# Inverse units of a chunked DeltaNet scan: level masks ahead on GpSimd, products carried by ScalarE, products and Relus spread over steps

## The chip, the cores and the metric

One core of one Trainium2 chip runs the whole kernel. The metric is the device time of one execution in microseconds (us), before and after the change. TensorE (PE) multiplies matrices into PSUM; VectorE (DVE), ScalarE (ACT) and GpSimd (POOL) work elementwise; SyncE (SP) and others issue the transfers. Each engine runs its own queue in order and waits on semaphores for the others.

## What is computed

One layer of a hybrid backbone over 128 context and 512 latent tokens in fp32: a first SwiGLU feed-forward net, a mixer with two head groups (gated DeltaNet and differential attention), the output projection, a second feed-forward net and a final norm. The change lies in the gated DeltaNet, in the part that solves the triangular system of each chunk:

```python
kk = jnp.einsum('bhncd,bhnsd->bhncs', kc, kc)
a_mat = jnp.where(strict, bc[..., :, None] * kk * decay, 0.0) + jnp.eye(CHUNK, dtype=jnp.float32)
rhs = jnp.concatenate([bc[..., None] * vc, (bc * jnp.exp(gc))[..., None] * kc], axis=-1)
sol = lax.linalg.triangular_solve(a_mat, rhs, left_side=True, lower=True, unit_diagonal=True)
...
qk = jnp.where(incl, jnp.einsum('bhncd,bhnsd->bhncs', qc, kc) * decay, 0.0)
```

There are 8 heads, two scan directions, and 5 token tiles of 128 (one of context, four latent).

## The kernel before

The kernel runs in stages: first feed-forward net, input projection and convolution, attention units, then **inverse units**, the scan (with parts of the output projection between), and the second feed-forward net. The inverse units lie between about 815 and 989 us.

An inverse unit makes the inverse of the 128x128 matrices of one token tile and four heads; both directions share it, since the strictly lower part serves one and the strictly upper part the other. There are 10 units u. Each goes through 20 steps k = 0 to 19, and starts at global step `MAKE_START[u]` (0, 4, 8, 13, 20, 24, 28, 33, 40, 44). Four sets of buffers c = u % 4 (`m_t`, `x_w`, `t_cols`, `tt_cols`; the last two sets have the name `spare` in the trace) and two PSUM banks each are used in turn, r = u // 4. `make_schedule` yields, for every global step, the events of that step with k None (attention tail, k and v transposed, scan beginnings) and then the steps of the units in order of u. All four engines write their queues by this one schedule; it sets the order within a queue, and semaphores (`t_pe`, `t_dve`, `t_act`, `t_pool`, with `PE_T`, `DVE_T`, `ACT_T`, `POOL_T` counts a unit) do the rest.

The steps of a unit before the change:

- k = 0: ScalarE fills `tt_cols` with beta (L1269, 4 instructions). k = 1: ScalarE's Relu of the decay rows of both directions, which a transfer brought (L1277, 4 for `x_w`, 4 for `t_cols`).
- k = 2: GpSimd adds the two (L2286); TensorE computes k*k and q*k of four heads (`products`, L2860). k = 3: ScalarE's exponential (L1282). k = 4: GpSimd multiplies beta in (L2289).
- k = 5: VectorE multiplies the products by the decays, into `m_t` (L2094) and `p_all` (L2096). k = 6: ScalarE copies the 32x32 diagonal blocks of `m_t` to `x_w[:, 1]` (L1286).
- k = 7: VectorE makes the inverse of level 0 (L2100, L2103), the transpose (L2114) and the two masked sides (L2116).
- Levels n = 1 to 4, k = 6 + 2n and 7 + 2n: TensorE multiplies the blocks with one side (`inner_first`, L2869, into PSUM); VectorE masks the product with the level's pattern into `x_w[:, 2]` (L2107); TensorE multiplies it with the other side (`inner_second`, L2876); VectorE subtracts it (L2111), transposes (L2114) and masks the sides (L2116).
- k = 16 to 19: the levels of 32 and 64 columns (`outer_first` L2884, `outer_own` L2896, `outer_second` L2902, `outer_turned` L2909, `last_first` L2920, `last_second` L2928), with ScalarE's negated copies (L1290, L1293), VectorE's L2120 and ScalarE's copies to `t_all` (L1297, L1303).

SyncE brings the decay rows of the next unit of a buffer set (`decays_spread`, L684) when the old unit is done. From global step 49 on GpSimd also masks the inverses for the scan (L2254, L2262), and from 54 on ScalarE prepares the scan (L1225) and the Silu of z (L1256, with table loads).

## Time and profile before

| | before |
|---|---|
| median of 3 runs | 1546.77 us (1543.21 to 1547.66) |
| the profiled execution | 1546.29 us, its span 1544.5 us |
| TensorE busy | 1458.2 us (94%) |
| VectorE busy | 1009.0 us (65%) |
| ScalarE busy | 620.6 us (40%) |
| GpSimd busy | 107.1 us (7%) |

The shares are means over stages. A stretch has to be read by itself: its busy times first, then what each engine waited for last. Times in the rows are microseconds from the start of the span, unless marked ns.

### The profile page before, as it was taken

How to read it: one execution, taken by the hardware profiler on the slowest of the kernel's cores; microseconds unless marked ns; L12 is line 12 of the kernel's file. 1: busy time of each engine (PE TensorE's matmuls, PEld its weight loads, DVE VectorE, ACT ScalarE, POOL GpSimd, SP SyncE). 2: the span in 40 equal slices, each digit the busy share in tenths (PEclk: the TensorE clock that was granted, in tenths of full speed). 3: DMA queues.
4: the chain of work that ended last, by engine and by line, in shares of the span. 5: the costliest groups of instructions: out<-in, count | busy, mean ns of one | idle time of the engine just before them, and what ended most of it. 6: DMA issues, size and time to landing. Idle time of an engine off the chain costs nothing.

```text
span 1544.5 us, 31492 instructions
## 1 busy us (share of the span) xinstructions
PE 1458.2 (94%) x12718; PEld 1350.8 (87%) x12718; DVE 1009.0 (65%) x1893; ACT 620.6 (40%) x1240; POOL 107.1 (7%) x88
## 2 busy tenths in 40 slices
PE   7899999999999999999996777899999999999998
PEld 2899999999999999887785556799999999998886
DVE  4977777777465747552886675478877777753333
ACT  4522222221122533442556555554544444444223
POOL 0000000000000000020002113553000000000000
PEclk9999999999999999998998776999999999999999
DMA  9344454445244222212101110111122223222222
GB/s 346 104 143 150 139 159 149 149 137 163 95 137 143 76 68 69 55 55 56 42 1 63 45 39 11 36 56 55 55 69 82 81 86 91 82 68 69 82 69 96
DMA packets 174589, 141.70 MB, mean 92 GB/s; under 512 B 8464, under 2 KB 156437, under 8 KB 173461
## 3 DMA queue, kind: packets, MB, share of 16 engines
q1 hardware_dynamic: 151652, 117.63, 24.5%
q10 hardware_dynamic: 22833, 22.59, 4.7%
q8 instruction: 77, 1.26, 0.3%
q14 instruction: 27, 0.22, 0.0%
HBM read 136.75 MB, written 3.45 MB: 91 GB/s over the span
## 4 chain that ended last, share of the span: by engine, by line
PE 83%; DVE 10%; issue 2%; ACT 2%; SPq 1%; DMA 1%; DVEq 0%; ACTq 0%
PE ps L2317 15%; PE ps L2318 14%; PE ps L2319 14%; PE ps L2469 5%; PE ps L2467 5%; PE ps L2468 5%; PE ps L2539 3%; PE ps L2537 3%; PE ps L2538 3%; PE ps L2959 1%; PE ps L2747 1%; PE ps L2768 1%; PE ps L2973 1%; PE ps L2944 1%; DVE tt_cols L2116 1%
## 5 line engine op out<-in xcount | busy, mean ns | idle before, releaser
L2317 PE MATMUL ps<-h_hi,w_lo 128*128 128x320 f32 x1152 | 366.5, 318 | 12.2 <-DVE h_lo L1445 4.5
L2318 PE MATMUL ps<-h_lo,w_hi 128*128 128x320 f32 x1152 | 358.5, 311 | 0.0
L2319 PE MATMUL ps<-h_hi,w_hi 128*128 128x320 f32 x1152 | 358.3, 311 | 0.0
L1398 DVE TENSOR_TENSOR w_lo<-w_raw,w_hi 128x1024 fp32r<-128x1024 f32 x120 | 148.1, 1236 | 233.3 <-ACT w_hi L742 233.0
L2317 PEld LDWEIGHTS ps<-h_hi,w_lo 128*128 128x128 f32 x1152 | 218.5, 190 | 19.6 <-issue 8.1
L2318 PEld LDWEIGHTS ps<-h_lo,w_hi 128*128 128x128 f32 x1152 | 218.9, 190 | 0.8 <-issue 0.2
L2319 PEld LDWEIGHTS ps<-h_hi,w_hi 128*128 128x128 f32 x1152 | 218.5, 190 | 0.0
L742 ACT CAST w_hi<-w_raw 128x1024 fp32r<-128x1024 f32 x120 | 125.5, 1047 | 198.8 <-PE ps L2319 109.3
L1532 DVE SCALAR_TENSOR_TENSOR ada_acc<-ada_ffn,cond,ada_acc 128x256 f32<-128x256 f32 x392 | 161.8, 479 | 1.2
L2317 PE MATMUL ps<-act_hi,w_lo 128*128 128x320 f32 (+1 forms) x352 | 108.9, 309 | 2.1 <-DVE mods L1561 2.1
L2318 PE MATMUL ps<-act_lo,w_hi 128*128 128x320 f32 (+1 forms) x352 | 108.5, 308 | 0.0
L2319 PE MATMUL ps<-act_hi,w_hi 128*128 128x320 f32 (+1 forms) x352 | 108.5, 308 | 0.0
L2467 PE MATMUL ps<-h_hi,w_lo 128*128 128x320 f32 x304 | 94.0, 309 | 0.6 <-ACT sumsq L905 0.6
L2469 PE MATMUL ps<-h_hi,w_hi 128*128 128x320 f32 x304 | 94.1, 310 | 0.0
L2468 PE MATMUL ps<-h_lo,w_hi 128*128 128x320 f32 x304 | 93.9, 309 | 0.0
L2537 PE MATMUL ps<-w_hi,act_hi 128*128 128x512 f32 x220 | 87.4, 397 | 0.0
L2539 PE MATMUL ps<-w_hi,act_lo 128*128 128x512 f32 x220 | 86.8, 395 | 0.0
L2538 PE MATMUL ps<-w_lo,act_lo 128*128 128x512 f32 x220 | 86.8, 394 | 0.0
L835 ACT CAST act_hi<-scratch 128x640 f32 (+1 forms) x22 | 16.0, 728 | 148.4 <-DVE scratch L1587 148.4
L2317 PEld LDWEIGHTS ps<-act_hi,w_lo 128*128 128x128 f32 x352 | 66.1, 188 | 2.4 <-issue 2.3
L2318 PEld LDWEIGHTS ps<-act_lo,w_hi 128*128 128x128 f32 x352 | 66.1, 188 | 0.1
L2319 PEld LDWEIGHTS ps<-act_hi,w_hi 128*128 128x128 f32 x352 | 66.1, 188 | 0.0
(425 smaller groups left out, 2909.2 us busy)
## 6 DMA issues: line engine op xcount, KB each, us to landing
w_raw<-in_w_ffn_in SPq DMA_DIRECT2D x64, 512.0 KB, 3.9
w_raw<-in_w_ffn_out SPq DMA_DIRECT2D x44, 512.0 KB, 3.7
ada_ffn<-in_w_ada ACTq DMA_DIRECT2D x43, 512.0 KB, 4.0
w_raw<-in_w_in SPq DMA_DIRECT2D x28, 512.0 KB, 3.7
ada_ffn<-in_w_ffn_in SPq DMA_DIRECT2D x20, 512.0 KB, 3.8
ada_k<-in_w_ada SPq DMA_DIRECT2D x8, 1024.0 KB, 10.6
ada_ffn<-in_w_ada SPq DMA_DIRECT2D x13, 512.0 KB, 3.4
w_raw<-in_w_out SPq DMA_DIRECT2D x8, 512.0 KB, 3.4
```

What stands on the lines that cost most here:

```text
L742: nc.scalar.copy(w_hi[s if slot is None else slot], w_raw[s][:]).then_inc(w_hi_ready, 1)
L1398: nc.vector.tensor_tensor(w_lo[at], w_raw[s][:], w_hi[at].bitcast(F32), ALU.subtract)\
L1532: ins = nc.vector.scalar_tensor_tensor(a, w, col, a, op0=ALU.mult, op1=ALU.add)
L2317: nc.tensor.matmul(out, lo, xh, start=start, stop=False)
L2318: nc.tensor.matmul(out, hi, xl, start=False, stop=False)
L2319: return nc.tensor.matmul(out, hi, xh, start=False, stop=stop)
L2467: nc.tensor.matmul(out, lo, xh, start=start and k == 0, stop=False, skip_group_check=not start)
L2468: nc.tensor.matmul(out, hi, xl, start=False, stop=False, skip_group_check=not start)
L2469: ins = nc.tensor.matmul(out, hi, xh, start=False, stop=k == 3, skip_group_check=not start)
L2537: nc.tensor.matmul(out, lo, wh, start=first, stop=False)
L2538: nc.tensor.matmul(out, hi, wl, start=False, stop=False)
L2539: ins = nc.tensor.matmul(out, hi, wh, start=False, stop=last)
```

## The change

`MAKE_START` and the 20 steps stay. The change

- moves TensorE's `products` from one lump in step 2 to one head in each of the steps 1 to 4,
- moves the second half of the Relus from step 1 to step 2, the exponential from step 3 to step 4, and `p_all` (L2096) from step 5 to step 6,
- lets ScalarE copy the diagonal blocks to `t_cols[:, 2]`, and lets GpSimd multiply them in step 6 with the patterns of levels 1 and 2, and 3 and 4, into `x_w[:, 0:4]` (two instructions),
- lets `inner_first` read those masked blocks, so that its product needs no mask. ScalarE copies it from PSUM to `t_cols[:, 3]` in steps 8, 10, 12 and 14, and VectorE's L2107 is gone.

```diff
 Z_TOTAL = [sum(Z_FIRST[:v + 1]) + sum(Z_SECOND[:v + 1]) for v in range(len(Z_FIRST))]
 Z_DONE = [min(v for v, n in enumerate(Z_TOTAL) if n >= 4 * g + 4) for g in range(2 * HB)]
 
-PE_T, DVE_T, ACT_T, POOL_T = 15, 23, 9, 2
+PE_T, DVE_T, ACT_T, POOL_T = 15, 19, 13, 4
 MAKE_ORDER = [0, 1, 4, 2, 3]
 OUT_ORDER = [0, 2, 3, 1, 4]
 OUT_EARLY = 3
...
             i = CONST_NAMES.index("pack0") * P + PACKED.index(name) * SUB
             return cst[:, i:i + SUB][:, None, :].broadcast_to([P, n, SUB])
 
+        def packed_pair(name, n):
+            i = CONST_NAMES.index("pack0") * P + PACKED.index(name) * SUB
+            return cst[:, i:i + 2 * SUB].rearrange("p (l n) -> p l n", n=SUB)[:, :, None, :].broadcast_to([P, 2, n, SUB])
+
         def unit_ident(a):
             i = CONST_NAMES.index("pack0") * P
             return cst[a:a + SUB, i:i + SUB]
...
                     ins.then_inc(t_act[c], 1)
                 if k == 1:
                     act.wait_ge(chain_in[c], 32 * r + 32)
-                    for d, x in ((0, x_w[c]), (1, t_cols[c])):
-                        q = 8 * d + 4 * g
-                        for h in range(4):
-                            ins = nc.scalar.activation(x[:, h, :], x[:, h, :], ACT.Relu,
-                                                       bias=gc[:, t, q + h:q + h + 1], scale=-1.0)
-                        ins.then_inc(t_act[c], 1)
-                if k == 3:
+                if k in (1, 2):
+                    d, x = ((0, x_w[c]), (1, t_cols[c]))[k - 1]
+                    q = 8 * d + 4 * g
+                    for h in range(4):
+                        ins = nc.scalar.activation(x[:, h, :], x[:, h, :], ACT.Relu,
+                                                   bias=gc[:, t, q + h:q + h + 1], scale=-1.0)
+                    ins.then_inc(t_act[c], 1)
+                if k == 4:
                     act.wait_ge(t_pool[c], r * POOL_T + 1)
                     nc.scalar.activation(x_w[c][:], x_w[c][:], ACT.Exp, scale=-1.0).then_inc(t_act[c], 1)
                 if k == 6:
-                    act.wait_ge(t_dve[c], r * DVE_T + 2)
+                    act.wait_ge(t_dve[c], r * DVE_T + 1)
                     for a in range(0, P, SUB):
-                        ins = nc.scalar.copy(heads4(x_w[c][a:a + SUB, 1, :], SUB), m_t[c][a:a + SUB, :, a:a + SUB])
+                        ins = nc.scalar.copy(heads4(t_cols[c][a:a + SUB, 2, :], SUB), m_t[c][a:a + SUB, :, a:a + SUB])
                     ins.then_inc(t_act[c], 1)
+                if k in (8, 10, 12, 14):
+                    act.wait_ge(t_pe[c], r * PE_T + k - 6)
+                    nc.scalar.copy(t_cols[c][:, 3, :], ps[:, 2 * c, 0:P]).then_inc(t_act[c], 1)
                 if k == 16:
                     act.wait_ge(t_pe[c], r * PE_T + 10)
                     nc.scalar.activation(x_w[c][:, 2, :], ps[:, 2 * c, 0:P], ACT.Copy, scale=-1.0).then_inc(t_act[c], 1)
...
                     act.wait_ge(t_pe[c], r * PE_T + 14)
                     nc.scalar.activation(x_w[c][:, 2:4, :].rearrange("p a n -> p (a n)"), ps[:, 2 * c, 0:256],
                                          ACT.Copy, scale=-1.0).then_inc(t_act[c], 1)
-                    act.wait_ge(t_dve[c], r * DVE_T + 23)
+                    act.wait_ge(t_dve[c], r * DVE_T + 19)
                     for a in range(0, P, DK):
                         ins = nc.scalar.copy(heads4(t_all[a:a + DK, t, g, :], P)[:, :, a:a + DK],
                                              heads4(ps[a:a + DK, 2 * c + 1, 256:512], DK))
...
                 nc.vector.tensor_tensor(out, out if s in (0, 3, 4) else oq[b], ps[:, 4 + b, 256:512], ALU.add).then_inc(c_dve[b], 1)
 
 
+            def by_pair(x):
+                return x.rearrange("p (h e) n -> p e h n", e=2)
+
+            def by_pair_of(x):
+                return x.rearrange("p e (h n) -> p e h n", n=P)
+
             for k, c, r, t, g in make_schedule():
                 if k is None:
                     if c == 4:
...
                 if k == 5:
                     dve.wait_ge(t_pe[c], pe0 + 1)
                     dve.wait_ge(t_pool[c], r * POOL_T + 2)
-                    for_heads = [x.rearrange("p (h e) n -> p e h n", e=2)
-                                 for x in (m_t[c][:], tt_cols[c][:], heads4(p_all[:, t, g, :], P), x_w[c][:])]
-                    nc.vector.tensor_tensor(for_heads[0], ps[:, bank:bank + 2, 256:512].rearrange("p e (h n) -> p e h n", n=P),
-                                            for_heads[1], ALU.mult).then_inc(t_dve[c], 1)
-                    nc.vector.tensor_tensor(for_heads[2], ps[:, bank:bank + 2, 0:256].rearrange("p e (h n) -> p e h n", n=P),
-                                            for_heads[3], ALU.mult).then_inc(t_dve[c], 1)
+                    nc.vector.tensor_tensor(by_pair(m_t[c][:]), by_pair_of(ps[:, bank:bank + 2, 256:512]), by_pair(tt_cols[c][:]),
+                                            ALU.mult).then_inc(t_dve[c], 1)
+                if k == 6:
+                    nc.vector.tensor_tensor(by_pair(heads4(p_all[:, t, g, :], P)), by_pair_of(ps[:, bank:bank + 2, 0:256]),
+                                            by_pair(x_w[c][:]), ALU.mult).then_inc(t_dve[c], 1)
                 if k == 7:
                     dve.wait_ge(t_act[c], act0 + 5)
-                    nc.vector.tensor_tensor(heads4(t_now, SUB), heads4(x_w[c][:, 1, :], SUB), packed("level0", 4),
+                    nc.vector.tensor_tensor(heads4(t_now, SUB), heads4(t_cols[c][:, 2, :], SUB), packed("level0", 4),
                                             ALU.mult).then_inc(t_dve[c], 1)
                     dve.wait_ge(t_dve[c], dve0 + 3)
                     nc.vector.tensor_tensor(heads4(t_now, SUB), heads4(t_now, SUB), packed("ident", 4), ALU.add).then_inc(t_dve[c], 1)
                 n, part = divmod(k - 6, 2)
-                if 1 <= n <= 4 and part == 0:
-                    dve.wait_ge(t_pe[c], pe0 + 2 * n)
-                    nc.vector.tensor_tensor(heads4(x_c, SUB), heads4(ps[:, bank, 0:P], SUB), packed(f"level{n}", 4),
-                                            ALU.mult).then_inc(t_dve[c], 1)
                 if 1 <= n <= 4 and part == 1:
                     dve.wait_ge(t_pe[c], pe0 + 1 + 2 * n)
                     nc.vector.tensor_tensor(t_now, t_now, ps[:, bank + 1, 0:P], ALU.subtract).then_inc(t_dve[c], 1)
                 if 0 <= n <= 4 and part == 1:
-                    dve.wait_ge(t_dve[c], dve0 + 4 + 4 * n)
+                    dve.wait_ge(t_dve[c], dve0 + 4 + 3 * n)
                     nc.vector.transpose(t_cols[c][:, 0, :], t_now).then_inc(t_dve[c], 1)
-                    dve.wait_ge(t_dve[c], dve0 + 5 + 4 * n)
+                    dve.wait_ge(t_dve[c], dve0 + 5 + 3 * n)
                     nc.vector.tensor_tensor(subs(t_sides), subs(t_pair), packed(f"sides{n + 1}", 8), ALU.mult).then_inc(t_dve[c], 1)
                 if k == 17:
                     dve.wait_ge(t_pe[c], pe0 + 13)
...
                 if k == 2:
                     pool.wait_ge(t_act[c], r * ACT_T + 3)
                     nc.gpsimd.tensor_tensor(x_w[c][:], x_w[c][:], t_cols[c][:], ALU.add).then_inc(t_pool[c], 1)
+                if k == 6:
+                    pool.wait_ge(t_act[c], r * ACT_T + 5)
+                    pool.wait_ge(t_dve[c], r * DVE_T + 2)
+                    for n in (1, 3):
+                        nc.gpsimd.tensor_tensor(x_w[c][:, n - 1:n + 1, :].rearrange("p l (h n) -> p l h n", n=SUB),
+                                                t_cols[c][:, 2:3, :].rearrange("p l (h n) -> p l h n", n=SUB)
+                                                .broadcast_to([P, 2, 4, SUB]),
+                                                packed_pair(f"level{n}", 4), ALU.mult).then_inc(t_pool[c], 1)
                 if k == 4:
                     pool.wait_ge(t_act[c], r * ACT_T + 4)
                     nc.gpsimd.tensor_tensor(tt_cols[c][:], tt_cols[c][:], x_w[c][:], ALU.mult).then_inc(t_pool[c], 1)
...
                 rows = slice((h % 2) * DK, (h % 2) * DK + DK)
                 return pre[rows, which + 2 * g + h // 2, t * P:(t + 1) * P]
 
-            def products(t, g, c):
-
-                for h in range(4):
-                    rows = slice((h % 2) * DK, (h % 2) * DK + DK)
-                    at = 2 * g + h // 2
-                    both = pre[rows, at:at + 5:4, t * P:(t + 1) * P]
-                    out = heads4(ps[:, 2 * c + h % 2, :], P)[:, h // 2:h // 2 + 3:2, :]
-                    ins = nc.tensor.matmul(out, qk(t, g, h, 4), both, start=True, stop=True)
-                ins.then_inc(t_pe[c], 1)
+            def products(t, g, c, h):
+
+                rows = slice((h % 2) * DK, (h % 2) * DK + DK)
+                at = 2 * g + h // 2
+                both = pre[rows, at:at + 5:4, t * P:(t + 1) * P]
+                out = heads4(ps[:, 2 * c + h % 2, :], P)[:, h // 2:h // 2 + 3:2, :]
+                ins = nc.tensor.matmul(out, qk(t, g, h, 4), both, start=True, stop=True)
+                if h == 3:
+                    ins.then_inc(t_pe[c], 1)
 
             def blocks_of(x, a, h):
                 return x[a:a + SUB, h * SUB:(h + 1) * SUB]
 
-            def inner_first(c):
+            def inner_first(c, n):
                 for h in range(4):
                     for a in range(0, P, SUB):
-                        ins = nc.tensor.matmul(blocks_of(ps[:, 2 * c, 0:P], a, h), blocks_of(x_w[c][:, 1, :], a, h),
+                        ins = nc.tensor.matmul(blocks_of(ps[:, 2 * c, 0:P], a, h), blocks_of(x_w[c][:, n - 1, :], a, h),
                                                blocks_of(tt_cols[c][:, 0, :], a, h), start=True, stop=True)
                 ins.then_inc(t_pe[c], 1)
 
             def inner_second(c):
                 for h in range(4):
                     for a in range(0, P, SUB):
-                        ins = nc.tensor.matmul(blocks_of(ps[:, 2 * c + 1, 0:P], a, h), blocks_of(x_w[c][:, 2, :], a, h),
+                        ins = nc.tensor.matmul(blocks_of(ps[:, 2 * c + 1, 0:P], a, h), blocks_of(t_cols[c][:, 3, :], a, h),
                                                blocks_of(tt_cols[c][:, 1, :], a, h), start=True, stop=True)
                 ins.then_inc(t_pe[c], 1)
 
...
                         attention_part(n // 2, [n % 2])
                     continue
                 pe0, dve0, act0 = r * PE_T, r * DVE_T, r * ACT_T
-                if k == 2:
+                if k == 1:
                     if r >= 1:
                         pe.wait_ge(t_act[c], act0)
                     elif c >= 1:
                         pe.wait_ge(kv_copied, 4 if c == 1 else 2 * NT + 2)
-                    products(t, g, c)
+                if 1 <= k <= 4:
+                    products(t, g, c, k - 1)
                 n, part = divmod(k - 6, 2)
                 if 1 <= n <= 4 and part == 0:
-                    pe.wait_ge(t_dve[c], dve0 + 2 + 4 * n)
-                    inner_first(c)
+                    pe.wait_ge(t_dve[c], dve0 + 3 + 3 * n)
+                    pe.wait_ge(t_pool[c], r * POOL_T + 3 + n // 3)
+                    inner_first(c, n)
                 if 1 <= n <= 4 and part == 1:
-                    pe.wait_ge(t_dve[c], dve0 + 3 + 4 * n)
+                    pe.wait_ge(t_act[c], act0 + 5 + n)
                     inner_second(c)
                 if k == 16:
-                    pe.wait_ge(t_dve[c], dve0 + 22)
+                    pe.wait_ge(t_dve[c], dve0 + 18)
                     outer_first(c)
                     outer_own(c)
                 if k == 17:
-                    pe.wait_ge(t_act[c], act0 + 6)
+                    pe.wait_ge(t_act[c], act0 + 10)
                     pe.wait_ge(t_pe[c], pe0 + 11)
                     outer_second(c)
                     pe.wait_ge(t_pe[c], pe0 + 12)
                     outer_turned(c)
                 if k == 18:
-                    pe.wait_ge(t_dve[c], dve0 + 23)
+                    pe.wait_ge(t_dve[c], dve0 + 19)
                     last_first(c)
                 if k == 19:
-                    pe.wait_ge(t_act[c], act0 + 7)
+                    pe.wait_ge(t_act[c], act0 + 11)
                     last_second(c)
 
             attention_part(1, [1])
```

## Rows read from the trace of the kernel before

**Rows 1.** Stretches: length; busy (x) PE, PEld, DVE, ACT, POOL; clock; DMA share; GB/s.
```profile
832.00:989.00 157.00, 114.00 (x4103) 92.39 (x4102) 96.00 (x243) 84.14 (x247) 40.68 (x32) 0.71 0.12 37
952.00:976.00 24.00, 21.76 (x568) 20.35 (x568) 10.22 (x30) 13.09 (x36) 5.03 (x5) 0.73 0.01 3
1100.00:1200.00 100.00, 98.10 (x666) 97.44 (x665) 80.26 (x124) 50.14 (x77) 0.00 (x0) 1.00 0.21 60
```

**Rows 2.** VectorE's waits, 832 to 989 us: waiter, releaser, total us, times, longest.
```profile
DVE t_cols L2111 <- PE ps L2876: 14.9, 10, 3.9
DVE spare L2107 <- PE ps L2869: 12.5, 11, 2.4
DVE spare L2111 <- PE ps L2876: 8.3, 6, 2.5
DVE x_w L2107 <- PE ps L2869: 7.8, 8, 1.8
```

**Rows 3.** Groups by line, 832 to 989 us: count | busy us, mean ns | idle before.
```profile
L2116 DVE TENSOR_TENSOR tt_cols<-t_cols,cst 128x256 f32<-128x256 f32 x30 | 18.7, 625 | 1.0
...
L2116 DVE TENSOR_TENSOR spare<-spare,cst 128x256 f32<-128x256 f32 x20 | 11.6, 579 | 0.7
...
L2107 DVE TENSOR_TENSOR x_w<-ps,cst 128x128 f32<-128x128 f32 x24 | 6.7, 285 | 8.0 <-PE ps L2869 7.8
...
L2107 DVE TENSOR_TENSOR spare<-ps,cst 128x128 f32<-128x128 f32 x16 | 4.6, 289 | 12.5 <-PE ps L2869 12.5
...
L1290 ACT ACTIVATE x_w<-ps 128x128 f32<-128x128 f32 x6 | 1.7, 277 | 9.3 <-PE ps L2884 9.3
```

**Rows 4.** Timeline, VectorE and TensorE, around 899 us: start, length, engine, line.
```profile
899.27 0.29 DVE L2107 TENSOR_TENSOR x_w<-ps,cst 128x128 f32<-128x128 f32 x1 [0.39 <-PE ps L2869]
899.57 0.29 DVE L2111 TENSOR_TENSOR t_cols<-t_cols,ps 128x128 f32<-128x128 f32 x1
...
899.02 1.10 PE L2876 MATMUL ps<-tt_cols,x_w 32*32 32x32 f32 x64
```

**Rows 5.** Timeline, VectorE and TensorE, 901 to 904 us, with a step 5.
```profile
901.24 0.42 DVE L2116 TENSOR_TENSOR tt_cols<-t_cols,cst 128x256 f32<-128x256 f32 x1
...
902.18 0.68 DVE L2096 TENSOR_TENSOR p_all<-ps,spare 128x512 f32<-128x512 f32 x1
902.78 0.48 DVE L2107 TENSOR_TENSOR x_w<-ps,cst 128x128 f32<-128x128 f32 x2
903.83 0.29 DVE L2111 TENSOR_TENSOR t_cols<-t_cols,ps 128x128 f32<-128x128 f32 x1 [0.57 <-PE ps L2876]
...
901.72 0.65 PE L2869 MATMUL ps<-tt_cols,x_w 32*32 32x32 f32 x32 [0.35 <-DVE tt_cols L2116]
903.12 1.08 PE L2876 MATMUL ps<-tt_cols,x_w 32*32 32x32 f32 x64 [0.74 <-DVE x_w L2107]
```

**Rows 6.** Timeline, TensorE and VectorE, a lump of products and the wait behind it.
```profile
872.69 2.08 PE L2860 MATMUL ps<-pre 64*128 64x256 f32 x8
...
876.37 0.29 DVE L2111 TENSOR_TENSOR spare<-spare,ps 128x128 f32<-128x128 f32 x1 [2.47 <-PE ps L2876]
```

**Rows 7.** Timeline, GpSimd and VectorE, 906 to 910 us.
```profile
906.66 1.27 POOL L2286 TENSOR_TENSOR spare<-spare 128x512 f32<-128x512 f32 x1 [8.26 <-ACT spare L1277]
...
906.84 1.37 DVE L2116 TENSOR_TENSOR spare<-spare,cst 128x256 f32<-128x256 f32 x1
```

**Rows 8.** Timeline, ScalarE: Relus, diagonal copies, and its queue before the scan.
```profile
823.53 1.26 ACT L1277 ACTIVATE t_cols<-t_cols,gc 128x128 f32<-128x128 f32 x4
...
883.37 1.22 ACT L1286 COPY x_w<-m_t 32x128 f32<-32x128 f32 x4
...
951.26 3.93 ACT L1225 ACTIVATE square<-k_tok,ekg 128x64 f32<-128x64 f32 x16
...
959.13 1.28 ACT L770 ACT_TABLE_LOAD   x1
```

**Rows 9.** The chain, 818 to 823 us: start, length, what.
```profile
818.95 3.37 DMA x_w<-decay_store
```

## Prediction

> **What bounds the kernel now.** I read the busy shares per stretch first. In a stretch that nothing here touches (1100 to 1200 us) TensorE is busy 98.1 of 100 us; the kernel is bound there by matmuls. In the stretch of the inverse units, 832 to 989 us, no engine is: TensorE 114.0 of 157 us, VectorE 96.0, ScalarE 84.1, GpSimd 40.7, and the granted clock is 0.71 on the mean, a mix of both levels [rows 1]. So this stretch is bound by latency: each of the four queues runs in order, step by step through the same schedule, and waits for its neighbours. What is saved on that round comes off the end one for one, because TensorE's dense work starts when it is over.
>
> Then VectorE's waits in it. 19 waits for the first product of a level (L2869) before the level mask L2107 come to 20.3 us, 16 for the second product (L2876) before the subtraction L2111 to 23.2 us; the longest waits of the two kinds are 2.4 and 3.9 us [rows 2]. Within the stretch 952 to 976 us TensorE is busy 21.8 of 24 us [rows 1]: it is the bound there, and no edit of this change shortens its work.
>
> **Part 1: the level masks leave VectorE.** 24 + 16 = 40 instructions L2107, 6.7 + 4.6 = 11.3 us busy, go away. What takes their place in the chain is a ScalarE copy of 128x128 from PSUM; the same shape from the same banks is L1290, 277 ns against 285 to 289 ns [rows 3]. The hop itself thus costs the same, if ScalarE is free. Is 11.3 us the gain? No, and one pair of steps shows it. VectorE masks the younger unit at 899.27 and subtracts for the older at 899.57; the older unit's second product started at 899.02, behind the first product of the younger [rows 4]. TensorE takes the products in order (first a, first b, second a), so with no mask VectorE would wait for second a, to about 899.6. Gain: nothing. The mask filled a gap.
>
> It gains where L2094/L2096 (step 5 of a young unit) stand ahead of the masks. The older units' masked sides end at 901.66 (901.24 + 0.42). VectorE runs L2096 at 902.18, both masks at 902.78, and only then can the two second products run (903.12 for 1.08 us), so L2111 starts at 903.83. The last first product had started at 901.72 and took 0.65 [rows 5]. With a copy by ScalarE the second product can run at 902.37, take about half of 1.08, and L2111 follows L2096 directly, at 902.86: 0.97 us less. Units 1 to 9 have such a step. Worked the same way, the gains are 0.8, 1.0, 1.2, 0.3, 0.9, 1.0, 0.6, 0.2 and 0.7 us: 6.7 us; the small ones are those where TensorE's own queue is the later one. In two more global steps (20 and 40) a wait before L2107 holds up L2100 to L2116 of a younger unit, up to the 2.4 us of rows 2; TensorE and the copy then become next, and 0.5 us each is left: 1.0 us.
>
> **Part 2: the products, one head per step.** Now 8 matmul records of step 2 stand in one lump. At 872.69 they take 2.08 us at the low clock level, and VectorE waits 2.47 us for a second product behind them, until 876.37 [rows 6]. A quarter stays in each step: 2.08 - 0.52 = 1.56 us less where the lump is on the path. I find it there for 4 of 10 units (the fifth, sixth, ninth and tenth); for the others TensorE would have waited for VectorE anyway. 4 x 1.5 = 6.0 us. For the sixth and the tenth the next to be late is ScalarE, which I allow for in part 4.
>
> **Part 3: the level masks on GpSimd.** Each unit adds two instructions of 128x256 (20 in all). The trace has no such shape on GpSimd; the nearest is 128x512 at 1.27 us [rows 7]. By columns it would be 0.64 us, and at the most 1.27. I take 0.65, since the same engine streams half the elements; the pair is then 1.3 us a unit, 13 us in all (upper end 25). GpSimd has room (40.7 of 157 us [rows 1]). Their queue: the add L2286 of the next unit, in the same step, stands behind the masks, which wait for ScalarE's diagonal copy and L2096; its result is wanted two steps later, so that costs nothing. The masks L2254 of the scan also stand behind them, with several us to spare before TensorE reads them. The first product of level 1 waits for the first mask: when the diagonal copy ends, VectorE needs L2100, L2103, L2114 and L2116 (three of 128x128 at 0.28 to 0.31 and one at 0.42, some 1.3 us) for the other operand, so the mask at 0.65 is in time.
>
> What does cost is this: L2116, which reads two tiles of SBUF, took 1.37 us from 906.84 while GpSimd's L2286 ran from 906.66 to 907.93 [rows 7]. The 50 L2116 take 18.7 + 11.6 = 30.3 us [rows 3] against 50 x 0.42 = 21.0, with 0.42 for a free one [rows 5]: 9 us lost so in about 33 of the 40.7 us of GpSimd work (the rest lies behind them). 13 us more of it at the same rate is 3.6 us, of which I put 70% on the path: 2.5 us. The ends are 0 (they fall in VectorE's idle time) and 7 us (25 us of GpSimd work, all on the path).
>
> The Trainium skill, page "SBUF — State Buffer", section "SBUF: two separate sides", says that a VectorE instruction with two SBUF inputs and a GpSimd instruction that reads SBUF exclude each other for their whole length. The trace agrees: 1.37 us, ended just after GpSimd's end.
>
> **Part 4: ScalarE's queue.** It gets 40 copies, 40 x 0.277 = 11.1 us, to 95 of 157 us. The copies wait for TensorE, and behind each wait stand the exponential, the diagonal copies and the Relus of younger units in the same step. In front of them stand lumps: four Relus 1.26 us, four diagonal copies 1.22 us [rows 8]. The change halves the Relu lump (8 instructions to 4 + 4), so one lump and not two is in front of a copy. In most steps the copy's product is later than the lump. In global steps 26/27 and 46/47 it isn't: the copies of step 18, the diagonal copies and the Relus come to over 3 us, so that the copy for the unit at step 14 is late by 1 to 2 us. For these and scattered cases I take 1.5 us. The ends are 0 and the lateness of the rival below.
>
> The Relu waits for the decay rows, whose transfer took 3.37 us in the first unit [rows 9] and is issued when the old unit of that buffer is done. By the timeline the time from there to the Relu is in some units little longer than that; if it shrinks below, the wait is ScalarE's, ahead of copies. The ends are 0 and 3 x 1 us, and I take 0.5.
>
> A new wait at the end: 16 activations, a table load, four Silus and another table load run from 951.26 to 960.41 without a stop [rows 8]. Now copies stand between them, and the last copies and the negation of the ninth unit come after the second table load. From the end of the 16 activations (951.26 + 3.93) to 960.41 are 5.2 us, and that much may now lie between the copies of the ninth unit's last level and its negation. TensorE has about as much work of its own in between (it is busy 21.8 of 24 us there [rows 1]). The ends are 0 and 5.2; I take 0.3, near the lower one.
>
> **Part 5: moves with one answer.** The second Relu moves to step 2 and the exponential to step 4: there GpSimd's multiplication must end before L2094 in step 5. The exponential, one instruction shorter than the four Relus' 1.26, and GpSimd's 1.27 are under 2.5 us, against a step of 2.7 us (157 us for 58 steps): hidden, at the price of 0.3 us in a lone unit, which is in the 0.8 of unit 1. L2096 moves to step 6: no time by itself, it fills the gap left by the masks. At the start ScalarE's rounding for the attention tail comes 1.26 us earlier, since four Relus [rows 8] now stand behind it, and VectorE is waiting for it: gain 1.0 us (ends 0 and 1.26).
>
> **The sum.** Gains 6.7 + 1.0 + 6.0 + 1.0 = 14.7; losses 2.5 + 1.5 + 0.5 + 0.3 = 4.8; net 9.9. The profiled execution took 1546.3 us (its span 1544.5), 0.5 below the median of 1546.77, which is nothing. 1546.3 - 9.9 = 1536.4. The steps I worked singly assume that all queues keep their phase, and some of the four lumps may turn out to be hidden; I forecast 1537.5.
>
> **Rivals.**
> - **VectorE waits for TensorE instead.** The pattern of rows 4 holds nearly everywhere: second products are late by themselves, and the 20.3 us of waits before L2107 reappear before L2111. For it: TensorE is the busiest of the four [rows 1]. Against it: rows 5. Then only the lumps gain, two of the four (3.0), with the start 1.0, less 2.5 on GpSimd: 1546.3 - 1.5 = 1544.8.
> - **GpSimd takes back what VectorE gains.** Masks of 1.27 us each, and every unit's own L2100 or L2116 waits for them, since they start on the same event: 10 x 0.7 more than I took, 1536.4 + 7 = 1543.4. The skill's page "Perfetto Trace Analysis", section "Optimizing Scalar/DVE Operations", says that moving work from VectorE to GpSimd might not help because they share a port. By that rule the time would be that of this rival; rows 7 bear it out for single instructions, while the GpSimd share in rows 1 speaks against it for the sum.
> - **ScalarE becomes late (slower).** One lump (1.22 or 1.26 us) in front of the copy in the 20 levels that no other unit's work covers: 20 x 1.25 = 25 us, against the 9.9. That gives 1546.3 + 15 = 1561; with 0.9 us each, 1554. It decides above 9.9/20 = 0.5 us of mean lateness. For it: before, ScalarE was free to lag, and nearly no chain went through it. Against it: it idles 73 of 157 us.
> - **The clock.** TensorE fell to the low level after its pauses in this stretch (mean 0.71). Shorter pauses could raise it, more and shorter ones lower it: 3 us to either side, part of the range.
>
> **Chances.** Forecast 0.60 (1530 to 1542), TensorE rival 0.15, GpSimd rival 0.12, ScalarE rival 0.13. A measurement of this kernel can tell about 0.3% (4.6 us) from no change: faster is below 1542.1, slower above 1551.4. Faster: 0.60 and a little of the GpSimd rival, 0.64. Slower 0.12. Same 0.24. The range 1530 to 1549 leaves out the ScalarE case and a few at the low end (no cost on GpSimd and a better clock).
>
> **What would show it.** L2107 gone; waits of VectorE for L2876 at 30 us or more, but under the old sum of 43.5; L1290-like copies of 0.28 us on ScalarE with little idle time charged to ScalarE by TensorE (under 5 us); the new GpSimd form at 0.65 us; L2860's matmuls in groups of two; more of L2116 above 1 us (some 15, 11 before); the dense work from about 979 on, where it is 989 now. I am wrong if TensorE's waits for ScalarE are above 10 us, or if the new GpSimd form takes over 1 us.

## Result, and the profile of the changed kernel

The changed kernel takes 1558.32 us (median of 5 runs, 1555.38 to 1559.88), the kernel before on the same chip 1546.77 us (5 runs). The ratio is 1.0064, with a 95% interval of 1.0038 to 1.0089: slower by some 11.5 us, where 1537.5 us was forecast. Both the sign and the range were wrong.

First the page of the changed kernel: the busy time of each engine over the whole span.

```profile
PE 1484.9 (95%) x12718; PEld 1364.6 (88%) x12718; DVE 1001.0 (64%) x1853; ACT 629.6 (40%) x1280; POOL 122.0 (8%) x108
```

Then the stretches, with the columns of [rows 1]. The unit stretch now ends about 1001 us, where the scan's first product starts at 1000.73; before it started at 988.74.

```profile
832.00:1001.00 169.00, 142.46 (x4093) 107.23 (x4094) 85.67 (x195) 89.89 (x276) 53.48 (x50) 0.58 0.11 34
1100.00:1200.00 100.00, 97.09 (x654) 95.75 (x653) 78.83 (x132) 50.72 (x82) 0.00 (x0) 1.00 0.23 67
```

The dense stretch is as in [rows 1]. The 12 us came in the unit stretch, and there VectorE's work went down as intended (96.0 us to 85.7, in a longer stretch), while TensorE's went up by 28 us with no more instructions (4103 matmul records before, 4093 now), and the granted clock fell from 0.71 to 0.58 on the mean (0.5 is the low level, 1.2 GHz, and 1.0 the high one, 2.4 GHz).

The groups by line of that stretch (count | busy us, mean ns | idle before) say which work grew. L2876 is now the unit's products, L2113/L2116 (before L2100/L2103) the level-0 step, L2125 (before L2116) the masked sides, L2300 the new masks, L1295 the new copies.

```profile
L2876 PE MATMUL ps<-pre 64*128 64x256 f32 x66 | 40.2, 711 | 0.0
L2125 DVE TENSOR_TENSOR tt_cols<-t_cols,cst 128x256 f32<-128x256 f32 x30 | 17.9, 596 | 1.0
...
L2300 POOL TENSOR_TENSOR x_w<-t_cols,cst 128x256 f32<-128x256 f32 x11 | 7.9, 737 | 23.5 <-DVE p_all L2109 13.1 <-ACT t_cols L1291 10.4
...
L1295 ACT COPY t_cols<-ps 128x128 f32<-128x128 f32 x24 | 6.3, 264 | 29.2 <-PE ps L2886 29.1
...
L2113 DVE TENSOR_TENSOR t_cols<-t_cols,cst 128x128 f32<-128x128 f32 x5 | 3.6, 711 | 0.0
```

The same kind of row for the products of the kernel before reads:

```profile
L2860 PE MATMUL ps<-pre 64*128 64x256 f32 x72 | 17.6, 636 | 0.0
```

So about the same matmuls keep TensorE busy for 40.2 us, not 17.6. Each takes little longer (711 against 636 ns, means over both clock levels): what changed is that they no longer run beside each other. The chain that ended last, summed by line over 832 to 1001 us, gives the line 16.3% of 169 us, 27.5 us; before, L2860 had 5.0% of 157 us, 7.9 us. These 19.7 us more on the chain are more than the whole loss, but they are not the whole account: the first and second products of the levels (L2886 and L2893, before L2869 and L2876) went from 24.2 to 31.9 us on it, and VectorE's lines gave way. The chain now runs more through TensorE altogether. First the changed kernel, then the kernel before:

```profile
by line: PE ps L2876 16.3%; PE ps L2893 9.7%; PE ps L2886 9.2%; DVE tt_cols L2125 7.3%; PE ps L2937 5.8%; issue 4.5%; PE ps L2976 4.3%; DVE t_cols L2123 3.8%; PE ps L2945 3.2%; PE ps L2926 3.0%; PE ps L2919 2.7%; DVE t_cols L2120 2.6%; PE p
```
```profile
by line: issue 9.2%; DVE tt_cols L2116 8.9%; PE ps L2876 8.1%; PE ps L2869 7.3%; DVE spare L2116 5.3%; DVE t_cols L2114 5.2%; PE ps L2860 5.0%; PE ps L2959 4.6%; PE ps L2928 3.8%; PE ps L2920 3.4%; DVE t_cols L2111 3.2%; DVE p_all L2096 2.7
```

One step in the timeline of the changed kernel (start, length, engine, line) shows a single head:

```profile
905.49 0.27 ACT L1295 COPY t_cols<-ps 128x128 f32<-128x128 f32 x1 [1.27 <-PE ps L2886]
...
905.78 0.65 PE L2886 MATMUL ps<-tt_cols,x_w 32*32 32x32 f32 x32 [0.35 <-DVE tt_cols L2125]
...
906.36 1.22 PE L2876 MATMUL ps<-pre 64*128 64x256 f32 x2
906.49 0.27 ACT L1295 COPY t_cols<-ps 128x128 f32<-128x128 f32 x1 [0.73 <-PE ps L2886]
...
907.51 0.70 PE L2893 MATMUL ps<-tt_cols,t_cols 32*32 32x32 f32 x36
```

ScalarE has carried both units' first products by 906.76. The second products (L2893) start at 907.51, behind one head of another unit that holds TensorE for 1.15 us. A lone head stands so in four steps of every unit.

Last, the waits (waiter, releaser, total us, times, longest): VectorE's for the second product, and all that TensorE's matmuls wait for ScalarE's copies.

```profile
DVE t_cols L2120 <- PE ps L2893: 33.0, 15, 5.0
DVE spare L2120 <- PE ps L2893: 20.9, 10, 4.4
```
```profile
PE ps L2893 <- ACT spare L1295: 0.4, 2, 0.2
```

53.9 us, against 20.3 + 23.2 = 43.5 us for both kinds of wait in [rows 2]. ScalarE is hardly late: beside these 0.4 us TensorE's weight loads, which overlap its matmuls, wait 2.6 us for the copies.

### The profile page after: what moved, and what is told of

Same layout as the page of the kernel before. It is cut to its first block, busy times and chain, and to the rows that moved or that the text cites. A ratio compares the mean times of both kernels' runs of the same rounds, so it can differ in the third digit from the quotient of the medians.

```text
span 1556.5 us, 31562 instructions
## 1 busy us (share of the span) xinstructions
PE 1484.9 (95%) x12718; PEld 1364.6 (88%) x12718; DVE 1001.0 (64%) x1853; ACT 629.6 (40%) x1280; POOL 122.0 (8%) x108
## 3 DMA queue, kind: packets, MB, share of 16 engines
q8 instruction: 77, 1.26, 0.3%
## 4 chain that ended last, share of the span: by engine, by line
PE 85%; DVE 8%; ACT 2%; issue 2%; SPq 1%; DMA 1%; DVEq 0%; ACTq 0%
PE ps L2334 15%; PE ps L2336 14%; PE ps L2335 14%; PE ps L2486 5%; PE ps L2484 5%; PE ps L2485 5%; PE ps L2556 3%; PE ps L2555 3%; PE ps L2554 3%; PE ps L2876 2%; PE ps L2976 1%; PE ps L2764 1%; PE ps L2785 1%; PE ps L2990 1%; PE ps L2893 1%
```

## The experiments

Each kernel ran on one chip beside the kernel before. On that chip it took 1547.41 us for the four kernels that take the change apart, 1550.09 us for the first pairs, the order, the masks ahead on VectorE and the unread masks, 1549.06 us for the same-half pairs and the other three kernels with pairs, and 1547.59 us for the last one. Ratios are to these, with 95% intervals, and kernels of different chips are compared by their ratios. A trace is of one run of a kernel and can lie some us off its median.

### The parts, one by one

**The products back in one lump**, everything else as changed:

```diff
-                if k == 1:
+                if k == 2:
                     if r >= 1:
...
-                if 1 <= k <= 4:
-                    products(t, g, c, k - 1)
+                if k == 2:
+                    for h in range(4):
+                        products(t, g, c, h)
```

> The changed kernel with the products of an inverse unit back in one lump in step 2; all else of the change stays. Theory P (packing): in the lump neighbouring heads lie in different halves of the rows of TensorE's array and run beside each other (8 records in 2.08 us before), a head alone takes 1.22 us, so four steps cost some 4.6 us a unit for 2.0. Then this kernel is faster than the changed one by 12 to 20 us: about 1538 to 1546 us, L2876's group falls from some 40 us back to 18. Theory C (the clock): the low level from 844 to 991 us comes from the new rhythm of masks and copies; then this kernel stays at the low level in most of that stretch and is at 1552 or above. Theory S (ScalarE or GpSimd late): no effect of the lump, 1555 to 1560.

1548.72 us, 1.0011 (0.9989 to 1.0034). One edit takes the changed kernel back to the time of before; the step between the two ratios is 0.53% or 8 us, and their intervals are apart. The rest of the change together can't be told from nothing.

**Only the spread**, in the kernel before:

```diff
-                if k == 2:
+                if k == 1:
...
-                    products(t, g, c)
+                if 1 <= k <= 4:
+                    products(t, g, c, k - 1)
```

> The kernel before with one edit: the products one head in each of the steps 1 to 4. Theory P: 10 units x 2.6 us more of TensorE time at the low clock level (half at the high one), of which half or more is on the path: 1556 to 1568 us, and the granted clock between 832 and 990 us falls. Theory C (the masks and copies set the clock): 1545 to 1550. The forecast's own reasoning (a quarter of the lump in each step) says 1540 to 1543.

1558.12 us, 1.0087 (1.0055 to 1.0119): the spread alone costs the whole loss. Its products keep TensorE busy as long as those of the changed kernel:

```profile
L2859 PE MATMUL ps<-pre 64*128 64x256 f32 x66 | 39.8, 704 | 0.0
```

**Only the masks and carries**: level masks on GpSimd in step 6, the copies L1295, L2096 moved to step 6; products in one lump, Relus and exponential where they were.

```diff
-                if 1 <= n <= 4 and part == 0:
-                    dve.wait_ge(t_pe[c], pe0 + 2 * n)
-                    nc.vector.tensor_tensor(heads4(x_c, SUB), heads4(ps[:, bank, 0:P], SUB), packed(f"level{n}", 4),
-                                            ALU.mult).then_inc(t_dve[c], 1)
+                if k == 6:
+                    pool.wait_ge(t_act[c], r * ACT_T + 5)
+                    pool.wait_ge(t_dve[c], r * DVE_T + 2)
+                    for n in (1, 3):
...
+                if k in (8, 10, 12, 14):
+                    nc.scalar.copy(t_cols[c][:, 3, :], ps[:, 2 * c, 0:P]).then_inc(t_act[c], 1)
```

> Only the mask part of the change: patterns applied ahead on GpSimd, products carried by ScalarE, L2096 in step 6; products in one lump in step 2, all Relus in step 1, exponential in step 3. The forecast's working gives 6.7 + 1.0 gained, about 4 lost on GpSimd and ScalarE: about 1543; if the Relu lump ahead of the copies matters, 1546 to 1552. Theory C and S: 1552 or more.

1551.64 us, 1.0031 (1.0011 to 1.005): slower by 4.8 us, where parts 1, 3 and 4 of the forecast made it a gain of 2.9. This is not the mask part alone. With the exponential still in step 3 it waits for GpSimd's add (L2294 here), which now stands behind the masks (L2299) in GpSimd's queue. Twice that is on the chain that ended last, so:

```profile
831.65 1.45 POOL x_w L2299 x2
833.11 1.41 POOL x_w L2294
834.54 0.63 ACT x_w L1286
```
```profile
ACT x_w L1286 <- POOL x_w L2294: 7.2, 3, 3.1
ACT spare L1286 <- POOL spare L2294: 3.5, 2, 3.1
```

The exponential waits 10.7 us so, against 0.3 us in the changed kernel, where it stands in step 4. The forecast had put this queueing at nothing, with the result wanted two steps later; that holds only with the later exponential.

**Only the moves** of the second Relu to step 2 and the exponential to step 4:

```diff
...
-                if k == 3:
+                if k == 4:
                     act.wait_ge(t_pool[c], r * POOL_T + 1)
...
```

> The kernel before with one edit: second half of the Relus in step 2, exponential in step 4. Theory P expects nearly nothing: 1545 to 1547 (a gain of up to 1.0 at the start). If the later exponential makes VectorE wait for GpSimd's multiplication in step 5, 1549 to 1553.

1549.12 us, 1.0007 (0.9984 to 1.003): not to be told from no change. In the profile the time from the first Relu to the first `m_t` product is 8.37 us, against 10.3 us in the kernel before; so the start is 1.9 us shorter (1.0 was forecast). The total shows no such gain, but its interval allows one of up to 2.5 us.

### Why a lone head costs so much

Heads h and h + 1 read different halves of the array's rows: `rows = slice((h % 2) * DK, ...)`, 0 to 63 and 64 to 127. A lone head leaves one half idle. The heads of one half also write one PSUM bank, `ps[:, 2 * c + h % 2]`, so in what follows a half of the rows and a PSUM bank always go together.

**Pairs in different halves**: heads 0 and 1 in step 2, 2 and 3 in step 3, the rest as changed.

```diff
-                if k == 1:
+                if k == 2:
                     if r >= 1:
...
-                if 1 <= k <= 4:
-                    products(t, g, c, k - 1)
+                if k in (2, 3):
+                    for h in (0, 1) if k == 2 else (2, 3):
+                        products(t, g, c, h)
```

> The changed kernel with the products in two pairs of neighbouring heads (0 and 1 in step 2, 2 and 3 in step 3) instead of four single heads. If what costs is a head standing alone (theory P), a pair takes about half of the lump, 1.1 us at the low level, and TensorE's time for L2876 falls from 40 to 16 to 18 us: 1544 to 1550 us, as the kernel with the lump or a little better. If spreading itself costs (breaking the round of first and second products in more steps, theory R), it lands between the lump and the changed kernel: 1552 to 1556.

1546.61 us, 0.9985 (0.9961 to 1.0009). In its timeline a pair takes what a lone head takes, and the next matmuls start as soon:

```profile
874.09 1.23 PE L2876 MATMUL ps<-pre 64*128 64x256 f32 x4
875.25 0.49 PE L2901 MATMUL ps<-spare 32*32 32x32 f32 x20
```

**Pairs in the same half** differ from that kernel by two numbers:

```diff
-                    for h in (0, 1) if k == 2 else (2, 3):
+                    for h in (0, 2) if k == 2 else (1, 3):
```

> As e3_pairs, but the pairs are heads 0 and 2 in step 2 and heads 1 and 3 in step 3: the two of a pair read the same half of the rows, while the other half stands idle. Number of steps and instructions are those of e3_pairs. Theory P (the two halves of TensorE's array work beside each other, and each half takes its two passes of a head one after the other): a pair takes 2.1 to 2.3 us at the low level, where the pair 0 and 1 takes 1.23, TensorE's time for the products is near 40 us as in the changed kernel, and the time is 6 to 12 us above e3_pairs: 1553 to 1560. Theory R (what costs is the number of pieces, not which heads): as e3_pairs, 1545 to 1549.

1555.79 us, 1.0045 (1.0028 to 1.0063): 0.60% or 9.2 us slower than the other pairing, with the same instructions in the same steps, and the intervals are apart. Its timeline:

```profile
875.28 2.07 PE L2876 MATMUL ps<-pre 64*128 64x256 f32 x4
877.29 1.01 PE L2945 MATMUL ps<-tt_cols,x_w 64*64 64x64 f32 x14
```

2.07 us, against 1.23. The 72 product records of this kernel between 832 and 1001 us keep TensorE busy for 32.4 us, the 64 of the other pairing for 16.4. Whether the shared rows or the shared bank makes the two heads of a pair wait for each other isn't separated by any run. One bank alone does not force it where the rows and the written partitions differ: the 32 products of 32x32 that `inner_first` writes into one bank took 0.65 us together, at 235 ns each on the mean.

**The order inside a lump**, in the kernel before:

```diff
-                for h in range(4):
+                for h in (0, 2, 1, 3):
```

> The kernel before with one edit: the heads of the lump in the order 0, 2, 1, 3, so that heads 0 and 2, and 1 and 3, which lie in the same half of the array's rows, follow each other; only 2 and 1 can run beside each other. Same work, same place, same step. Theory P: the lump takes some 3.4 us at the low level instead of 2.08 (three head times for two), L2860's spans from first to last grow by half, and the time by 2 to 6 us, as the lump is on the path for about 4 of 10 units: 1549 to 1553. If neighbouring heads don't run beside each other, nothing changes: 1546 to 1548.

1549.3 us, 1.0001 (0.9979 to 1.0023), and the lump takes 2.08 to 2.09 us as in [rows 6]. What this expected of a half left idle inside a lump was wrong: by these times each half works on its own heads as long as both have some queued. Of the pieces tried, only those that held heads of one half paid.

### Why the masks do not pay

**The patterns applied ahead by VectorE**: as the kernel with the lump, but no masks on GpSimd; VectorE applies level 1 in step 7 and levels 2 to 4 in step 8, one 128x384.

```diff
+                if k in (7, 8):
+                    lv = slice(0, 1) if k == 7 else slice(1, 4)
...
+                    nc.vector.tensor_tensor(x_w[c][:, lv, :].rearrange("p l (h n) -> p l h n", n=SUB),
...
-                if k == 6:
-                    pool.wait_ge(t_act[c], r * ACT_T + 5)
-                    pool.wait_ge(t_dve[c], r * DVE_T + 2)
-                    for n in (1, 3):
```

> The changed kernel with the lump back in step 2 (as e1_lump) and the patterns of levels 1 to 4 applied ahead by VectorE (one 128x128 in step 7, one 128x384 in step 8: some 0.28 + 0.56 us a unit) instead of GpSimd; ScalarE still carries the products. If GpSimd's lock is what eats the gain of the mask part (theory G; VectorE lost 5 to 6 us to it beyond before in e1_lump and e5_masks_only), this is faster than e1_lump by 2 to 4 us: 1543 to 1547. If the copies on ScalarE or TensorE's order are what limits it (theory T), it is the same as e1_lump or slower, since VectorE has 8.4 us more to do: 1548 to 1552.

1544.06 us, 0.9965 (0.9945 to 0.9985). By the ratios this is 0.46% or 7.1 us better than the same work on GpSimd (1.0011, its interval just apart from this one), although VectorE does more.

**GpSimd masks that nothing needs**, in the kernel before: 20 multiplications of 128x256 in step 6, whose results are written to free tiles and not read. (ScalarE's step 18, which writes one of these tiles, has to wait for them; the trace lists no such wait.)

```diff
+                if k == 6:
+                    pool.wait_ge(t_act[c], r * ACT_T + 5)
+                    pool.wait_ge(t_dve[c], r * DVE_T + 2)
+                    for n in (1, 3):
...
+                        nc.gpsimd.tensor_tensor(x_w[c][:, 0:4:3, :].rearrange("p l (h n) -> p l h n", n=SUB),
+                                                x_w[c][:, 1:2, :].rearrange("p l (h n) -> p l h n", n=SUB)
```

> The kernel before plus 20 GpSimd multiplications of 128x256 in step 6, whose results nobody reads: the cost of GpSimd's part of the change by itself. Theory G: VectorE's instructions with two operands in SBUF lose 4 to 6 us more, of which most is on the path: 1550 to 1554. The forecast's term was 2.5: 1549 to 1550. Theory T: under 1 us, 1546 to 1548.

1551.3 us, 1.0013 (0.9992 to 1.0035): 2 us, and the interval holds zero. Here too the exponential waits for the add behind the new work, 11.2 us in all. Where the new instructions land is seen in the groups by line; L2105 and L2108 are L2100 and L2103 of before, two tiles of SBUF in, which start on the same event as the new GpSimd work:

```profile
L2298 POOL TENSOR_TENSOR x_w<-x_w,cst 128x256 f32<-128x256 f32 x12 | 9.0, 748 | 27.6 <-ACT x_w L1290 27.1
...
L2105 DVE TENSOR_TENSOR t_cols<-x_w,cst 128x128 f32<-128x128 f32 x6 | 4.1, 690 | 0.1
L2108 DVE TENSOR_TENSOR t_cols<-t_cols,cst 128x128 f32<-128x128 f32 x6 | 4.4, 742 | 0.2
L2108 DVE TENSOR_TENSOR spare<-spare,cst 128x128 f32<-128x128 f32 x4 | 1.2, 291 | 0.1
```

Before, the first of them reads so:

```profile
L2100 DVE TENSOR_TENSOR t_cols<-x_w,cst 128x128 f32<-128x128 f32 x6 | 1.7, 284 | 0.1
```

### A version that beats both

Four more kernels use pairs in different halves. **The patterns ahead on VectorE, with pairs** (against the kernel with those patterns and the lump):

```diff
-                if k == 2:
-                    for h in range(4):
+                if k in (2, 3):
+                    for h in (0, 1) if k == 2 else (2, 3):
                         products(t, g, c, h)
```

> e8_ahead_on_vector (patterns ahead on VectorE, products carried by ScalarE, Relus and exponential moved) with the products in pairs 0 and 1, 2 and 3 as in e3_pairs. If the gains add (e8 was 5.4 us below before, pairs for lump gave 4 us with GpSimd's masks): 1537 to 1542. If TensorE's low clock takes them back: 1543 to 1547.

1542.11 us, 0.9945 (0.9924 to 0.9966), the lowest ratio of all: 8.5 us faster than before by the ratio, 7.0 us by the medians. The intervals of the next kernels overlap with this one, so that the order among them is open. Its products take 16.5 us, and the stretch 832 to 989 us reads:

```profile
832.00:989.00 157.00, 118.74 (x4130) 96.28 (x4131) 97.15 (x223) 94.77 (x295) 45.04 (x34) 0.70 0.13 37
```

**Only the pairs**, in the kernel before:

```diff
...
-                    products(t, g, c)
+                if k in (2, 3):
+                    for h in (0, 1) if k == 2 else (2, 3):
+                        products(t, g, c, h)
```

> The kernel before with one edit: products in pairs 0 and 1 in step 2, 2 and 3 in step 3. The forecast's idea of a lump on the path in 4 of 10 units, now with the right price: half of 2.08 taken off each, 4 us: 1542 to 1544. Theory P also allows no gain, where the second half is on the path of the next step: 1546 to 1548. Above 1550 would mean that any spreading costs.

1544.62 us, 0.9968 (0.9946 to 0.9991): splitting the lump is worth 5 us, if each piece keeps both halves. Three more comparisons of pairs with the lump go the same way: 4 us with the masks on GpSimd (0.9985 against 1.0011) and 3 us with the patterns on VectorE (0.9945 against 0.9965), where the intervals overlap, and 7.4 us with the moves (0.9959 against 1.0007, the kernel that follows), where they don't.

**Pairs and the moves of the Relu and the exponential**, masks on VectorE behind the products as before; against the kernel with the moves alone the edit is the one just shown:

> e11_before_pairs with the second Relus in step 2 and the exponential in step 4; the masks stay on VectorE behind the products. Against e10_vector_pairs it shows what carrying the products by ScalarE is worth once GpSimd is left alone. Theory M (the mask mostly filled gaps, forecast's rows 4): the difference is under 3 us, this one 1541 to 1546. If the mask part is worth the forecast's 7.7 us: this one 1545 to 1549 with e10 at 1538 to 1541.

1544.17 us, 0.9959 (0.9938 to 0.9979). The kernel with the lowest ratio against this one is what the carry by ScalarE brings when no mask is on GpSimd: 0.14%, 2.1 us (1544.17 less 1542.11), and the intervals overlap.

**GpSimd's masks later**: pairs; VectorE applies level 1 in step 7, GpSimd levels 2 to 4 as one 128x384 in step 8.

```diff
-                if k == 6:
+                if k == 8:
                     pool.wait_ge(t_act[c], r * ACT_T + 5)
-                    pool.wait_ge(t_dve[c], r * DVE_T + 2)
+                    pool.wait_ge(t_dve[c], r * DVE_T + 7)
...
```

> As e10_vector_pairs and e3_pairs, but the patterns are shared: VectorE applies level 1 (128x128, step 7), GpSimd applies levels 2 to 4 in one instruction of 128x384 in step 8, after VectorE's sides of level 0, wanted by TensorE only in step 10. So GpSimd does about the same streaming (some 1.0 us a unit for 1.5), but no longer starts on the event on which VectorE's level 0 starts. Theory E (the price of GpSimd's part is that collision and the wait for the first mask): close to e10, 1540 to 1544. Theory L (any GpSimd work beside VectorE's round costs by its lock): close to e3_pairs, 1545 to 1549.

1541.38 us, 0.9961 (0.9942 to 0.998). GpSimd's masks now take 10 instructions of 0.99 to 1.0 us, and L2113, the first of level 0, is free again:

```profile
L2113 DVE TENSOR_TENSOR t_cols<-t_cols,cst 128x128 f32<-128x128 f32 x5 | 1.4, 287 | 1.1 <-ACT t_cols L1291 1.1
```

L2116, the second, takes 681 ns on the mean for the five of the same tiles, but with no mask on GpSimd it is nearly the same (618 ns in the kernel with pairs and the patterns on VectorE). Between masks in step 6 (0.9985) and masks on VectorE (0.9945) this kernel lies nearer the latter. That speaks for more of GpSimd's cost from the place than from the work, but it isn't shown: the intervals of the three overlap in part, and the level-1 mask was moved to VectorE in the same edit.

## Why the prediction was wrong, step by step

**What bounds the stretch: right.** No engine fills it, and what is added there moves the end: the scan starts 12.0 us later and the span is 12.0 us longer (1556.5 against 1544.5).

**Part 2, the products: the step that failed.** It says "A quarter stays in each step: 2.08 - 0.52 = 1.56 us less where the lump is on the path". The lump of 2.08 us is two halves of the array working beside each other; a lone head takes 1.22 us at the low clock level, and the next matmul starts 1.15 us after it. So a step keeps over half of the lump, not a quarter, and there are four such steps a unit: 4 x 1.15 = 4.6 us of TensorE's queue for 2.08. What I priced at a gain of 6.0 us was a loss: from before to the spread alone +0.87% (13 us by the ratio, 10.7 us by the medians); from the changed kernel to the lump 0.53% less (8 us, 9.6 us by the medians). The lump-on-the-path reading itself is borne out: split into pieces that keep both halves (1.23 us each), the lump gives back 5 us (1.4 to 8.4 by the interval), where 6.0 was forecast for quarters. What should have stopped me stood in the trace of before: the lump of [rows 6] is eight matmuls in 2.08 us, and the group of L2860 has a mean of 636 ns for one, which makes 5.1 us of matmul time in 2.08 us of span. Work that overlaps itself can't be divided by its count. (A sum somewhat above the span is not the sign yet: the two records of a lone head, 2 x 711 ns, also exceed its 1.22 us. The lump's exceed it two and a half times.)

The Trainium skill, page "TensorEngine Tiling (Array Packing)", section "Key Properties", says that different tiles of the array can load weights and multiply in parallel. The trace agrees for the two halves of the rows: 1.23 us for a pair in different halves against 2.07 us in the same one.

**Part 1, masks off VectorE (+7.7 us): mostly not there.** The part called the mask a gap-filler in one pair of steps [rows 4] and counted gains in ten others. With the lump in place VectorE's waits for the second product were 25.8 + 17.2 = 43.0 us, against the sum of 43.5 before: what L2107 no longer waits for, L2120 does. That is the rival "VectorE waits for TensorE instead". Where no mask is on GpSimd, the carry brought 2.1 us, which can't be told from nothing. The waits, from the kernel with the lump:

```profile
DVE t_cols L2120 <- PE ps L2893: 25.8, 13, 5.0
DVE spare L2120 <- PE ps L2893: 17.2, 10, 2.9
```

**Part 3, GpSimd: the duration right, the cost mis-sized.** The new form took 0.74 to 0.80 us on the mean (0.65 forecast, bounds up to 1.27). The excess of the two-SBUF-input instructions of level 0 and of the sides over a free one, summed over the ten units, is 9.1 us in the kernel before, all in L2116; it is 12.9 us in the changed kernel, 15.4 with the lump and 15.0 with the unread masks. So 4 to 6 us more, near the 3.6 forecast, though kernels with no new work on GpSimd already vary from 8 to 12 us. But I put 70% of 3.6 on the path, spread at random, and it isn't: the masks start on the very event on which L2100 starts, so that 5.0 to 7.5 us of excess fall on level 0 of the units, where nothing had been blocked (0 to 2.0 us in the kernels without them). The forecast also put the add behind the masks at nothing; with the exponential in step 3 it held the exponential up for 10.7 us, with the exponential in step 4 for 0.3. Taking GpSimd out was worth 7.1 us with the lump and 6.2 us with pairs (0.9985 to 0.9945 of 1549), against the 2.5 forecast; that was the rival "GpSimd takes back what VectorE gains", which had the event ("they start on the same event") and nearly the size, 2.5 + 7 = 9.5 us. Its other half is not there: in no trace with step-6 masks does TensorE's list of waits name one for GpSimd. The unread masks cost 2 us (-1.2 to 5.4 by the interval), less than the 7.1, so that the collision alone may not be all of it; what the rest is wasn't found.

**Part 4, ScalarE: right in kind, too dear.** The copy takes 264 to 266 ns (277 forecast). TensorE's waits for it are 0.4 us in the changed kernel and 4.0 us with the lump, the longest of them 2.8 us; 1.5 was allowed for in the changed kernel, and the rival "ScalarE becomes late" is refuted by the 0.4. The kernel came out slower by a price of TensorE's that no rival named.

**Part 5, the start: right in kind, too small.** 1.9 us against 1.0, beyond the upper end of 1.26; the total doesn't resolve it.

**The clock: named, with the wrong size.** In 800 to 1020 us TensorE was at the low level (1.2 GHz) for 92 us in the kernel before, 143 in the changed one and in the spread alone, 140 with pairs in the same half, 126 with the first pairs, 130 with the patterns on VectorE and the lump (a profiled run of 1553 us, the slowest of its thirteen), 109 with the changed kernel's lump, 96 in the kernel with the lowest ratio, and from 89 to 123 in the other seven. The three that leave a half idle stand at the top; the others don't order by their times. A lone head at the high level costs 0.70 us and at the low level 1.22, so the two causes act together, and no run held one of them fixed.

The runs themselves say more than the forecast's 3 us. In the 107 runs of the kernel before, the time goes with the mean granted clock of the run: nine runs at 0.951 to 0.953 took 1553.6 to 1558.3 us, sixteen at 0.965 or more took 1540.8 to 1546.5. The changed kernel's five were granted 0.947 to 0.953, and the one at 0.953 took 1555.38 us. A straight line through the 107 (0.86 us less for each 0.001 of clock) puts the five only 0.3 us above it on the mean (four of them lie where the line is drawn on below its lowest clock, 0.951), and the spread alone and the pairs in the same half within 1 us of it, while the kernels with the pairs in different halves lie 1 to 5 us below. So at a like clock the changed kernel and the one before can't be told apart: nearly the whole loss comes together with the lower clock. The edits show that it is the pieces with heads of one half alone that bring it about. By which road, TensorE's longer queue or the longer time at the low level, stays open, since a longer stretch at the low level also lowers the mean. That a half-used array brings the low clock is a pattern of these runs and not shown by a test of its own.

Of the signs named, L2107 was gone, the new GpSimd form stayed below 1 us and TensorE's waits for ScalarE below 5 us, so neither of the two conditions for "I am wrong" was met. What spoke against the forecast were the waits above the old sum (53.9 us) and the dense work at 1001 instead of 979 us. The sign for part 3 failed too: 4 of the masked sides took over 1 us, not some 15 (10 in the trace of before, where the forecast counted 11), while level 0 was slowed.

## What to carry to other kernels

Before dividing a lump of matmuls, add up its single durations: if they exceed the span several times, the pieces overlap, and a piece must keep what overlaps together (here two heads in different row halves and PSUM banks). Before comparing two runs, look at the clock that each was granted. Before moving work to GpSimd, look at which VectorE instruction with two SBUF inputs starts on the same event, and put the GpSimd work two steps later or leave it on VectorE; look also at what stands behind it in GpSimd's queue. A sum of gains read step by step needs the same care for its prices as for its mechanisms: here the reading of the stretch was right, and the price of one piece turned the sign.

## What was unexpected of the hardware

- The product of one head (64 rows, 256 columns) costs the same alone as together with one on the other half: 1.22 and 1.23 us at the low clock level, 0.70 us both at the high one. Two on the same half cost 2.07 us (1.13 at the high level), as much as four on both halves (2.08 and 1.13).
- The order of the heads in a lump is of no account (2.08 to 2.09 us for 0, 2, 1, 3).
- TensorE was recorded busy for 142 of 169 us and was granted less clock (0.58) than when busy for 114 of 157 us (0.71); part of the longer busy time is the lower clock itself.
- Runs of one kernel on one chip differ by up to 16 us with the clock that they were granted: the kernel before took 1542.49 us at a mean of 0.967 and 1558.28 us at 0.953.
- GpSimd's multiplication of 128x256 took 0.74 to 0.80 us on the mean and of 128x384 0.99 to 1.0 us, against 1.27 us for 128x512 [rows 7].
